# A one-core decoder trunk: dilated scores taken four heads at a time, projection columns by token half, and attention steps moved

## The reference, cut to what matters

```python
D_MODEL, SEQ, DEPTH, HEAD_DIM = 1024, 256, 2, 64     # 16 heads: 8 causal (MoBA with one block), 8 dilated
def hybrid_layer(x, ...):                            # all float32, batch 1
    h = rms_norm(x, attn_norm)
    qa, ka, va, qd, kd, vd = split(h @ w_in)         # 1024 x 3072, six groups of 512 columns
    qa, ka, qd, kd = rope of each
    out_a = rms_norm(merge_heads(moba_attention(qa, ka, va)), moba_out_norm)
    out_d = rms_norm(merge_heads(dilated_attention(qd, kd, vd)), dil_out_norm)
    x = x + concatenate([out_a, out_d]) @ w_out
    h = rms_norm(x, mlp_norm)
    return x + square(relu(h @ w_up)) @ w_down       # D_FF = 4096
# output: rms_norm(x, final_norm) after DEPTH layers
```

## Time and profile before

| | |
|---|---|
| median of three runs | 599.85 us (599.79 to 599.92) |
| the profiled execution: its time, its span | 599.85 us, 598.1 us |
| busy share of the span: PE, PEld | 99%, 81% |
| DVE, ACT, POOL | 66%, 53%, 8% |
| mean DMA bandwidth | 174 GB/s |
| instructions | 8728 |

### The profile page before, as it was taken

The page is one execution under the profiler, slowest core; times in us unless marked ns, Lnnn a source line. Parts: engine busy times, 40 slices in busy tenths (PEclk is TensorE's granted clock), DMA queues, the critical chain, the costliest instruction groups (busy, mean ns, idle before and its releaser), DMA issues.

```text
span 598.1 us, 8728 instructions
## 1 busy us (share of the span) xinstructions
PE 589.3 (99%) x3066; PEld 485.0 (81%) x3066; DVE 393.9 (66%) x655; ACT 316.8 (53%) x536; POOL 46.5 (8%) x51
## 2 busy tenths in 40 slices
PE   8999999999999999999999999999999999999995
PEld 5877777788888888888888777878888888888884
DVE  5866958687755755656388478677875755755634
ACT  5747749475535435344284567674654435435322
POOL 0220230110000000000004013001100000000001
PEclk9999999999999999999999999999999999999999
DMA  8954344248665464564266434431877465465301
GB/s 303 354 212 142 141 141 142 71 140 276 220 222 196 151 236 174 169 250 143 71 209 212 141 140 142 133 112 45 269 249 249 141 219 201 149 224 188 105 0 70
DMA packets 58842, 104.00 MB, mean 174 GB/s; under 512 B 1808, under 2 KB 35264, under 8 KB 58816
## 3 DMA queue, kind: packets, MB, share of 16 engines
q1 hardware_dynamic: 58320, 102.87, 50.7%
q10 hardware_dynamic: 496, 0.81, 0.4%
HBM read 102.62 MB, written 1.05 MB: 173 GB/s over the span
## 4 chain that ended last, share of the span: by engine, by line
PE 98%; DVE 1%; issue 0%; POOLq 0%; POOL 0%; ACT 0%; DVEq 0%; ACTq 0%
PE psum L1051 20%; PE psum L892 20%; PE psum L894 19%; PE psum L893 19%; PE psum L1054 10%; PE psum L1008 2%; PE psum L1024 1%; PE psum L899 1%; PE psum L999 1%; PE psum L985 1%; PE psum L983 1%; PE psum L882 1%; PE psum L1027 1%; PE psum L914 1%; PE psum L920 0%; PE psum L923 0%
## 5 line engine op out<-in xcount | busy, mean ns | idle before, releaser
L611 DVE TENSOR_TENSOR w_lo<-raw,w_hi 128x1024 fp32r<-128x1024 f32 x188 | 229.4, 1256 | 51.4 <-ACT w_hi L447 51.4
L447 ACT CAST w_hi<-raw 128x1024 fp32r<-128x1024 f32 x188 | 187.0, 1049 | 3.0 <-DMA raw<-in_w_in 3.0
L1051 PE MATMUL psum<-xt,w_hi 128*128 128x512 f32 x512 | 160.8, 395 | 0.0
L892 PE MATMUL psum<-w_hi,ot_hi 128*128 128x512 f32 x320 | 127.5, 398 | 0.0
L894 PE MATMUL psum<-w_hi,ot_lo 128*128 128x512 f32 x320 | 125.0, 391 | 0.0
L893 PE MATMUL psum<-w_lo,ot_hi 128*128 128x512 f32 x320 | 124.9, 390 | 0.0
L1054 PEld LDWEIGHTS psum<-xt,w_lo 128*128 128x128 f32 x512 | 96.2, 188 | 22.3
L1054 PE MATMUL psum<-xt,w_lo 128*128 128x256 f32 x512 | 100.8, 278 | 0.0
L1051 PEld LDWEIGHTS psum<-xt,w_hi 128*128 128x128 f32 x512 | 80.3, 189 | 2.3
L558 ACT COPY up_cross<-psum 128x512 f32<-128x512 f32 x32 | 18.8, 588 | 118.8 <-PE psum L1054 118.8
L892 PE MATMUL psum<-w_hi,xt 128*128 128x512 f32 x180 | 74.3, 413 | 0.0
(11 more groups left out here) (85 smaller groups left out, 445.5 us busy)
## 6 DMA issues: line engine op xcount, KB each, us to landing
raw<-in_w_up SPq DMA_DIRECT2D x32, 1024.0 KB, 5.5
raw<-in_w_down SPq DMA_DIRECT2D x32, 1024.0 KB, 6.7
raw<-in_w_in SPq DMA_DIRECT2D x21, 1024.0 KB, 5.5
raw<-in_w_out SPq DMA_DIRECT2D x8, 1024.0 KB, 4.9
raw<-in_w_in SPq DMA_DIRECT2D x3, 512.0 KB, 7.8
raw<-in_w_in SPq DMA_DIRECT2D x4, 256.0 KB, 4.6
out<-x SPq DMA_DIRECT2D x3, 256.0 KB, 2.4
raw<-in_w_in ACTq DMA_DIRECT2D x2, 256.0 KB, 5.1
```

The lines of the kernel that those rows point to most:

```text
L447: act.copy(w_hi[:, slot, part], raw[:, slot, part]).then_inc(hi_done, 1)
L611: dve.tensor_tensor(w_lo[:, slot, part], raw[:, slot, part], w_hi[:, slot, part].bitcast(F32), ALU.subtract).then_inc(split_done, 1)
L892: pe.matmul(out, s_hi, m_hi, start=first, stop=False)
L1051: pe.matmul(up_banks[b][:, f, :], w_hi[:, slot, cols[f]], xt[:, k, :, :].rearrange("p a b -> p (a b)"), start=k == 0, stop=False)
```

## The change

The tables are rewritten, and `project_in` is reordered.
- Scores: dilated heads 0 to 3 in one go at step 22 and 4 to 7 at step 32 (before: two heads each at 23, 27, 31, 35). Heads 2, 3, 6 and 7 get banks 0 and 1.
- PV of pairs 0 and 1 together at step 32, just ahead of those scores (before: 31 and 35). PV of pairs 2 and 3 at 46, just ahead of the first causal scores (before at 41, the scores alone at 46).
- The sum of squares of the dilated output at 51 (before 45), in the bank of PV's products.
- Per-head work of heads 0 to 3 one step earlier, of heads 4 to 7 one step later. The probabilities of heads 0 to 7 are now transposed at 25, 27, 29, 31, 35, 37, 39, 41 (before 26 to 40, even steps). QKT is at 14, 15, 19, 20, 39, 41, 44, 47 (before 20 and 21 for 19 and 20).
- From group 1 on, a step takes two k for one token half: the first four steps of a group are t = 0, the last four t = 1, always in banks 2 and 3. Rope and v then follow per token half, four steps earlier for t = 0 than for both before. A new semaphore, `half_done`, tells that t = 0 of a group is complete. A unit of weights is wanted at step 8g + j instead of 8g + 2j, and released at 8g + 4 + j instead of 8g + 2j + 1. Some `hi` are one step later.

```diff
-QK_AT = {23 + 2 * h if h < 8 else 38 + h: h for h in range(N_HEADS)}
+QK_AT = {22 + 2 * h if h < 4 else 24 + 2 * h if h < 8 else 38 + h: h for h in range(N_HEADS)}
 NORM_AT = {s + 1: h for s, h in QK_AT.items()}
 PT_AT = {s + 3: h for s, h in QK_AT.items()}
-PV_AT = {31: (0,), 35: (1,), 41: (2, 3), 53: (4, 5), 57: (6, 7)}
-QK_PAIRS_AT = {23: (0,), 27: (2,), 31: (4,), 35: (6,), 46: (8, 10), 50: (12, 14)}
+PV_AT = {32: (0, 1), 46: (2, 3), 53: (4, 5), 57: (6, 7)}
+QK_PAIRS_AT = {22: (0, 2), 32: (4, 6), 46: (8, 10), 50: (12, 14)}
...
-QKT_AT = {14: 0, 15: 1, 20: 2, 21: 3, 39: 4, 41: 5, 44: 6, 47: 7}
-ROPE_AT = {8 * g + 8: g for g in ROPE_GROUPS}
-V_AT = {8 * g + 8: g for g in V_GROUPS}
+QKT_AT = {14: 0, 15: 1, 19: 2, 20: 3, 39: 4, 41: 5, 44: 6, 47: 7}
+ROPE_AT = {8: ((0, 0), (0, 1))} | {8 * g + 4 * t + 4: ((g, t),) for g in ROPE_GROUPS if g > 0 for t in range(TOK)}
+V_AT = {8 * g + 4 * t + 4: (g, t) for g in V_GROUPS for t in range(TOK)}
 TAIL = 56
-STAT_D = 45
+STAT_D = 51
...
-V_AT_LAST = max(V_AT)
-HI_AT = {s + int(s == V_AT_LAST): s // 2 + HI_AHEAD for s in range(0, 2 * ATT_UNITS, 2)}
+HI_AT = {s + int(s % 8 == 4 or s in V_AT): s // 2 + HI_AHEAD for s in range(0, 2 * ATT_UNITS, 2)}
...
-        early_banks = {8: banks[0], 9: banks[1], 12: banks[2], 13: banks[3]}
+        more_banks = {h: banks[h % 2] for h in (2, 3, 6, 7, 8, 9)} | {12: banks[2], 13: banks[3]}
...
+            def project_in(l, s):
+                g = s // 8
...
+                t, j = s % 8 // 4, s % 4
+                u = 4 * g + j
+                if t == 0:
+                    unit_ready(l, u // 2, u % 2)
...
+                if j == 0 and g - 1 in V_GROUPS:
+
+                    pe.wait_ge(v_done, l * 4 + t + 1)
+                elif j == 0 and g > 1:
+                    pe.wait_ge(rope_terms, l * 8 + 2 * ROPE_GROUPS[g - 1] + t + 1)
...
-                if h == SET_HEADS:
-                    pe.wait_ge(rope_terms, l * 8 + 8)
-                elif h == SET_HEADS + 2:
-                    pe.wait_ge(mean_done, l * STATS + ST_D + 1)
+                if h == 2:
+                    pe.wait_ge(rope_terms, l * 8 + 2)
...
-                elif h >= 2:
-                    pe.wait_ge(masked, l * N_HEADS + h)
+                elif h >= 4:
+                    pe.wait_ge(masked, l * N_HEADS + h - 2)
...
                 if s == STAT_D:
-                    pe.wait_ge(masked, l * N_HEADS + SET_HEADS)
-                    sum_squares(l, 0, stat_d)
+                    pe.wait_ge(o_split, l * PAIRS + SET_PAIRS)
+                    sum_squares(l, 0, stat)
```

More of the change, by code:

```diff
@@ L507, in _ @@
                     if s in V_AT:
-                        g = V_AT[s]
-                        act.wait_ge(weights_used, used(l, 4 * g + 3))
+                        g, t = V_AT[s]
+                        if t == 0:
+                            act.wait_ge(half_done, half_group(l, g))
+                        else:
+                            act.wait_ge(weights_used, used(l, 4 * g + 3))
                         act.wait_ge(rstd_done, l * STATS + ST_X + 1)
[L511 to L514, removed]
+                        act.activation(v[:, V_GROUPS[g], t, :], group_bank(g, t)[:, :], ACT.Copy,
+                                       scale=rstd[:, ST_X, t:t + 1]).then_inc(v_done, 1)
                     if s in QKT_AT:
@@ L658, in rope_products @@
                 j = ROPE_GROUPS[g]
-                dve.wait_ge(weights_used, used(l, 4 * g + 3))
+                if g > 0 and t == 0:
+                    dve.wait_ge(half_done, half_group(l, g))
+                else:
+                    dve.wait_ge(weights_used, used(l, 4 * g + 3))
                 dve.wait_ge(rope_scaled, l + 1)
@@ L725, in _ @@
                     if s == STAT_D + 1:
[L726 removed]
+                        o_mean(l, ST_D, stat)
                     if s in QK_AT:
@@ L742, in _ @@
                     if s in ROPE_AT:
-                        if ROPE_GROUPS[ROPE_AT[s]] == 0:
+                        if s == min(ROPE_AT):
                             scale_rope(l)
-                        for t in range(TOK):
-                            rope_products(l, ROPE_AT[s], t)
+                        for g, t in ROPE_AT[s]:
+                            rope_products(l, g, t)
                     if s % 2 == 1 and u < 2 * FIRST_UP + 1:
@@ new lines, in project_in @@
+                if j == 0 and g == 1 and l == 0:
+                    pe.wait_ge(gains_kept, 1)
+                if j == 0 and g - 1 in V_GROUPS:
+                    pe.wait_ge(v_done, l * 4 + t + 1)
+                elif j == 0 and g > 1:
+                    pe.wait_ge(rope_terms, l * 8 + 2 * ROPE_GROUPS[g - 1] + t + 1)
+                tok = slice(t * P, (t + 1) * P)
+                for k in (2 * j, 2 * j + 1):
+                    cols = slice((k % 4) * BANK, (k % 4 + 1) * BANK)
+                    last = three(group_bank(g, t)[:, :], xt[:, k, 0, tok], xt[:, k, 1, tok],
+                                 w_hi[:, u // 2 % RING, cols], w_lo[:, u // 2 % RING, cols], k == 0, k == KT - 1)
@@ L934, in project_in, with first_group @@
+                if t == 1:
+                    last.then_inc(weights_used, 1)
+                elif j == 3:
+                    last.then_inc(half_done, 1)
+            def first_group(l, u, k):
+                if l == 0 and k < 6:
                     first_project_in(k)
                     return
-                if s == 1:
+                cols = slice((k % 4) * BANK, (k % 4 + 1) * BANK)
+                if k == 1:
                     pe.wait_ge(first_lo_half, l)
-                elif s % 2 == 0:
-                    unit_ready(l, c, u % 2)
@@ L940, in project_in @@
[L940 to L948, removed]
+                elif k % 2 == 0:
+                    unit_ready(l, u // 2, u % 2)
+                pe.wait_ge(turned_lo, l * TRS + TR_X + k + 1)
@@ L949, in project_in @@
                 for t in range(TOK):
                     tok = slice(t * P, (t + 1) * P)
[L951 to L954, removed]
+                    last = three(group_bank(0, t)[:, :], xt[:, k, 0, tok], xt[:, k, 1, tok],
+                                 w_hi[:, u // 2 % RING, cols], w_lo[:, u // 2 % RING, cols], k == 0, k == KT - 1)
@@ L956, in project_out @@
+                if k % 2 == 1:
+                    last.then_inc(weights_used, 1)
             def project_out(l, acc, k, u, t, n, first, last):
```

32 lines of the change are left out of this document (19 added, 13 removed).

## The result

| | before | after |
|---|---|---|
| median, five runs each | 599.92 us (599.79 to 600.14) | 616.07 us (615.22 to 618.46) |
| the profiled execution: its time, its span | 599.85, 598.1 | 615.33, 613.6 |
| PE's clock, mean over the span | 0.998 | 0.992 |
| DVE, ACT, POOL busy | 66%, 53%, 8% | 65%, 52%, 8% |

The changed kernel takes 1.0275 times as long [1.0255 to 1.0296]: 16.1 us more, where 7.9 were forecast, and above the range. The helpers stand lower in the file now: L892 to L894 became L904 to L906, QKT's L999 is L1025, PT's L1008 is L1034, the QKT copy L519 is L528, the PT copy L526 is L535, `hi` L447 is L455, `lo` L611 is L620, the mask L734 is L746, the norm L641 is L650.

What follows compares the result with a forecast made beforehand. PE was taken as the bound, time being the sum of its intervals. Per layer 4.2 + 0.9 - 1.1 = +4.0 us, +7.9 for two layers on 599.85, gave 607.7 us (605.4 to 609.6; wider range 603.5 to 611).

Steps and rivals of the forecast that it cites:

- the prediction's own signs of being wrong: In the trace: no idle PE before PT, head 7's mask early, granted clock below 1, waits for `w_lo` or `probs_t`.
- What the breaks save: Per layer, PE's merged attention breaks and shared transposes save 1.1 us; 2.2 in all (2.0 to 2.6).
- The wait for the bank: At steps 39 and 41, PT waits for ACT's copy of the same step's QKT: 4.2 and 0.9 us.
- the least wait: PT's wait for the QKT copy with an idle ACT, expected at step 41: about 0.9 us (0.75 to 1.1).
- Rivals 1 and 2: 1: ACT in time at 39, both waits least, 601.3 us, chance 0.09. 2: PT doesn't stand behind copy, 597.6, chance 0.04.
- The long wait: PT at step 39 waits for ACT's copy, late behind DVE's mask of head 7: 4.2 us (3.3 to 4.8).
- O: Start of the last projection matmul (L894) before the break at step 32, from which times to step 39 were counted.
- So I cost the clock at nothing: During PE's idle time of some 4 us at step 39, the clock stays at 2.4 GHz; cost nothing.
- rival 3: The clock falls within the long wait at step 39: 1.8 us lost, twice, +3.6, 611.3; chance 0.10.
- The rest, at nothing, and what hides it: Weights, rope and v wanted earlier, PT at 37 (0 to 0.4 us) and other moved work cost PE nothing.
- The sum: Per layer 4.2 + 0.9 - 1.1 = +4.0 us; two layers +7.9 (5.5 to 9.8), giving 607.7.
- rival 4: Something costed at nothing also waits: +0.5 to +2 us more, within the range; part of the forecast's 0.77 chance.

Runs made afterwards that it cites:

- c3: c1 with `hi` of steps 34 and 38 one step later, `lo` of step 37 at 38, head 7's norm ahead of `lo` again: 598.43 us, 0.9972.
- b1: The kernel before with its QKT groups at 38 and 40 instead of 39 and 41, sharing steps with PT: 603.87 us, 1.0063.
- a4: The changed kernel with twelve unused matmuls on PE between QKT and PT in step 39: 612.36 us, 1.0204.
- a1: The changed kernel with QKT at 38 and 40 instead of 39 and 41, where there is no PT: 608.63 us, 1.0148.
- a2: The changed kernel with the one-step delay of `hi` kept to steps up to 48, as before the change: 615.43 us, 1.0265.
- a3: The changed kernel with DVE's norm of the dilated heads behind the `lo` of its step instead of ahead: 612.76 us, 1.0202.
- c1: Changed kernel, QKT at 20, 21, 42, 43, `hi` table as before from step 48, norm behind `lo` for heads 0, 1, 2, 5, 7: 600.14 us.

## Why the prediction was wrong

Its direction and its main mechanism held; its size was half. Two steps failed, the clock and the list of things at nothing. Two of the prediction's own signs of being wrong are in the trace: a granted clock of 0.50 behind the wait, and PT at 37 and 55 waiting for ACT's copies, `probs_t`. Point by point:

- **What the breaks save** was right. The two breaks of two PV and two score pairs cost 3.21 and 3.18 against 3.29, and the term of -1.1 per layer, which wasn't measured by itself, closes the account to 0.1. c3 shows most of it as time.
- **The wait for the bank** was right, and so was the least wait: 0.9 forecast, 0.92 at step 41 and in b1. Rivals 1 and 2 are out.
- **The long wait**, "4.2 us, 3.3 to 4.8", measured 4.74: right in mechanism, and small by 0.5. The mask of head 4 began at O + 2.83 (59.43, 62.26) where 2.8 was worked out. From there to the end of head 7's mask it took 14.0 us, not 12.0 and 0.9 for contention: the contention was 0.78 and 1.06, and it fell on the norms, not on `lo`, which ran at 1.21 and 1.22 each time. The prediction had looked for the POOL sum beside the only operation whose slow row it had. PE was itself 0.45 later at step 39 than forecast (74.08 is O + 14.65, not 14.2), by its wait at 37, which gave part of that back.
- **"So I cost the clock at nothing"** is the first step that failed. The prediction read 4.4 us of idle PE before the clock's fall in the earlier trace rows, estimated the idle time at 3.9, and gave the fall 0.10 (its rival 3). The clock fell 4.3 us after PE's last work, since the idle time was 4.58. By a4 that is 1.45 per layer, 2.9 in all; rival 3 had 3.6. The margin, 0.5 us, was smaller than the 0.6 by which the wait's own range went up: the step treated two numbers that lay closer than their errors as settled. And it took the 4.4 us of one row as a bound, where the clock of a1 and a2 then fell after less. The Trainium skill, "TensorE: Matmul & The Clock Gate", section "Why this matters for your kernels", had warned of just such a gap between bursts; the trace agrees (half clock in both layers behind 4.58 us), and the warning should have had most of the chance at a wait of this length.
- **"The rest, at nothing, and what hides it"** is the second. Of the list, the PT at 37 was named with 0 to 0.4, taken as 0, and measured 0.47; the PT at 31 wasn't listed and waited 0.29. Behind both is what the prediction had seen and not followed, that the exponent is bare when the norm comes right behind its mask: 3.49 us per head on DVE against 3.08 on PE. It counted this once, for head 5; heads 0 to 2 have it too, and the norm of head 3 then ran beside POOL (1.61 at 56.22). In a3, where `lo` hides the exponent, both waits are gone. The PT at 55 (0.62) wasn't listed at all. The text of the change says "some `hi` are one step later", and the prediction never followed that one (52 to 53) through ACT's queue. The QKT at 19 (0.54, first layer) was moved a step earlier, and its condition, rope's sum on POOL, wasn't dated; with QKT at 20 and 21, c1 and c3 don't have this wait. Together 3.3 us.
- **The sum**: forecast +7.9, measured +15.4 in the profiled execution. Of the 7.5 between them, 3.3 are waits costed at nothing, 2.9 the clock, and 1.1 the long wait; 0.2 is rounding. The median run adds 0.7, at a lower mean clock (0.990 against 0.992).
- The range ended at 611. Its upper end took in "the lower part of rival 3" but not rival 3 with even 1 us of rival 4, and both came, because one late DVE queue is behind the long wait and most of the small ones: they were added as if they were apart.

## What to carry to other kernels

When one queue feeds several waits, date every moved step in it, the ones off the path too; a wait that is forecast at several microseconds is a sign that the queue is late for its other customers too, and these costs come together. Two users of one PSUM bank in the same step cost a whole round trip even with idle engines (0.92 us here), and moving one of them leaves part of the wait while the engine that empties the bank is late (0.69 and 1.88 us in a1, for 4.74 and 0.92). If a forecast wait lies near the longest idle time that the trace shows at full clock, give the fall of the clock the larger chance, and price the work behind the wait at half rate.

## What the runs showed of the hardware

- **DVE's norm beside POOL.** The norm's two TENSOR_SCALARs took 0.55 alone, and 1.61 beside POOL's 1.3 us TENSOR_TENSOR (72.95 on DVE, 72.92 on POOL); at 65.06, where POOL's two sums lay beside them in part, 1.33. The earlier trace rows had shown this for `lo` only, 1.98 for 1.22. The Trainium skill, "SBUF — State Buffer", section "Who interferes with whom", names both: a `tensor_scalar` can enter a mode that takes the port pair that VectorE shares with GpSimd, an instruction with two inputs in SBUF needs that pair's read side, and whichever starts first holds the other up. The trace agrees for the norm: POOL's row starts 0.03 us ahead, and the norm takes 1.06 longer.
- **The clock fell in more ways than one.** After 4.3 us of idle PE in the changed kernel, as at the end of the trace before (4.4). In a2, with the same wait, after 2.2 us (74.2 to 76.4) in the first layer, and in a3, whose wait was 3.0, after 2.2 in the second (372.1 to 374.4). And also in a1, where PE was idle for only 0.69 and 1.88 us, some 4 us apart, with matmuls between, and only in the second of two like layers; and not in a4, which had 1.83 and 1.81 us idle, each in one piece. The low stretches lasted 3.4 us in the changed kernel's profile and in a1, and 6.8 us in a2. What decides between them wasn't tried. The five runs of the changed kernel scatter over 3.2 us; the four of a4, without the fall, over 0.3.
